# Sample attention values as 512-column products, and last expert products and final norm by thirds of tokens

## The reference, cut to what matters

```python
def mem_attend(q, mk, mv):
    s = jnp.einsum('bthd,bmhd->bhtm', q, mk.astype(q.dtype)).astype(jnp.float32) * (MEM_HEAD_DIM ** -0.5)
    p = jax.nn.softmax(s, axis=-1).astype(q.dtype)
    o = jnp.einsum('bhtm,bmhd->bthd', p, mv.astype(q.dtype))
    return o.reshape(q.shape[0], q.shape[1], MEM_Q)
```

```python
    x = x + peer(rmsnorm(x, norm_ffn_g), peer_w_q, peer_sub_keys, peer_u, peer_v)
...
def rmsnorm(x, g):
    xf = x.astype(jnp.float32)
    r = lax.rsqrt(jnp.mean(xf * xf, axis=-1, keepdims=True) + EPS)
    return (xf * r).astype(x.dtype) * g
```

## Time and profile before

| | us |
|---|---|
| median of three runs | 6134.89 |
| the profiled execution | 6135.75 |
| span of its records | 6134.0 |
| TensorE matmul busy | 5819.9 (95%) |
| VectorE busy | 3493.0 (57%) |
| ScalarE busy | 1329.1 (22%) |

### The profile page before, as it was taken

The page is one execution under the profiler, slowest core; times in us unless marked ns, Lnnn a source line. Parts: engine busy times, 40 slices in busy tenths (PEclk is TensorE's granted clock), DMA queues, the critical chain, the costliest instruction groups (busy, mean ns, idle before and its releaser), DMA issues. The chain is left out here.

```text
span 6134.0 us, 98920 instructions
## 1 busy us (share of the span) xinstructions
PE 5819.9 (95%) x37440; PEld 5687.3 (93%) x37440; DVE 3493.0 (57%) x8585; ACT 1329.1 (22%) x2383; POOL 875.0 (14%) x554
## 2 busy tenths in 40 slices
PE   8999999978887799899899999999999999999999
PEld 7999999878886599799899999999999999999998
DVE  3235300226664244599999998565565565565555
ACT  3113211213331013122233333121121121121121
POOL 0333223214332234133100000000000000000000
PEclk9999999979997799899999999999999999999999
DMA  4122222431110444211233333433333333333332
GB/s 153 59 73 94 97 90 94 145 111 35 35 35 14 144 148 125 75 59 48 80 149 146 142 141 139 136 87 101 83 87 100 83 90 98 83 92 96 83 92 69
DMA packets 706337, 584.63 MB, mean 95 GB/s; under 512 B 384664, under 2 KB 628376, under 8 KB 703189
## 3 DMA queue, kind: packets, MB, share of 16 engines
q1 hardware_dynamic: 663824, 425.64, 23.7%
q10 hardware_dynamic: 41184, 152.59, 7.0%
q0 software_dynamic: 1152, 4.19, 0.2%
HBM read 410.77 MB, written 171.59 MB: 95 GB/s over the span
## 5 line engine op out<-in xcount | busy, mean ns | idle before, releaser
L2959 DVE TENSOR_TENSOR yT<-yT,ex_y 128x352 f32<-128x352 f32 x1536 | 800.2, 521 | 918.6 <-PE ex_y L2851 918.6
L2213 PE MATMUL ea_banks<-h_high,ea_uT_high 128*128 128x352 f32 x3072 | 1013.8, 330 | 0.0
L2213 PE MATMUL ea_banks<-h_high,ea_uT_low 128*128 128x352 f32 x3072 | 991.8, 323 | 0.0
L2213 PE MATMUL ea_banks<-h_low,ea_uT_high 128*128 128x352 f32 x3072 | 991.6, 323 | 0.0
L2851 PE MATMUL ex_y<-ex_c_high,w_mb_high 128*128 128x352 f32 x3024 | 976.4, 323 | 3.7 <-DVE yT L2959 3.7
L2851 PE MATMUL ex_y<-ex_c_low,w_mb_high 128*128 128x352 f32 x3024 | 973.4, 322 | 0.0
L2851 PE MATMUL ex_y<-ex_c_high,w_mb_low 128*128 128x352 f32 x3024 | 972.2, 321 | 0.0
L120 PE MATMUL p_in<-h_high,w_in_high 128*128 128x352 f32 x2112 | 681.3, 323 | 0.0
L120 PE MATMUL p_in<-h_low,w_in_high 128*128 128x352 f32 x2112 | 676.9, 320 | 0.0
L120 PE MATMUL p_in<-h_high,w_in_low 128*128 128x352 f32 x2112 | 676.3, 320 | 0.0
L2213 PEld LDWEIGHTS ea_banks<-h_low,ea_uT_high 128*128 128x128 f32 x3072 | 584.4, 190 | 0.0
(11 more groups left out here) (470 smaller groups left out, 9851.5 us busy)
## 6 DMA issues: line engine op xcount, KB each, us to landing
ex_gate<-tmp_gates SPq DMA_DIRECT2D x128, 528.0 KB, 6.2
w_mb_raw<-in_peer_v SPq DMA_DIRECT2D x128, 512.0 KB, 5.6
ea_u_raw<-in_peer_u ACTq DMA_DIRECT2D x126, 512.0 KB, 3.3
w_in_raw<-in_w_in SPq DMA_DIRECT2D x88, 512.0 KB, 3.8
tmp_acts<-ea_coef ACTq DMA_DIRECT2D x64, 528.0 KB, 2.8
tmp_gates<-yT SPq DMA_DIRECT2D x11, 3072.0 KB, 9.0
tmp_gates<-sg_out SPq DMA_DIRECT2D x11, 3072.0 KB, 10.0
ex_kept<-tmp_acts SPq DMA_DIRECT2D x64, 528.0 KB, 6.9
```

Source lines behind the costliest of these rows:

```text
L2213: last = pe.matmul(acts.banks[:, n, 0:CH], a[:, c, :], b[:, c, chunk(n)], start=(c == 0 and a is acts.uT_high[s] and b is high), stop=(c = ...
L2959: dve.tensor_tensor(at, at, ps_y[:, n, 0:CH], ALU.add).then_inc(summed, 1)
```

## The change

In `attend`, the operands are exchanged. The cached values are the moving operand, 512 columns at a time, and the stationary operand is, for each sequence, a 128x128 block of probabilities that is zero outside that sequence's 16 rows (`s_pT` becomes [128, 8, 2, 128]; GpSimd zeroes it, VectorE copies the 16 columns of each sequence in). All 32 matmuls add into two banks of 128 rows by 1024 channels. The result then has rows of (sequence, head, token); it is copied to SBUF, transposed in 8 blocks, and 4 copies pick the 64 elements each that belong to a head.

In `experts`, the last pass takes its units chunk by chunk (all 8 channel blocks of 352 tokens, then the next chunk) and uses two banks in turn. The transposes of the final norm are put into it: a unit q of the first chunk is transposed in 3 pieces (128, 128 and 96 tokens) after unit q + 2, the second chunk's after units 15, 16 and 17, the third chunk's after unit 23. ScalarE squares each transposed tile with a running sum and takes its root, VectorE inverts and scales it between the sums of the next chunk, and SyncE stores it. `norm_rows_out` and its sums by matmul are gone, and with them a block.

```diff
-        s_pT = sb("s_pT", [P, MT, P])
+        s_pT = sb("s_pT", [P, NB, MT, P])
+        s_rows = sb("s_rows", [P, D])
...
-        s_values = banks[:, 6, 0:KT * NS].rearrange("p (c n) -> p c n", n=NS)
+        s_values = banks[:, 6:8, :]
+        s_columns = banks[:, 0:2, :].rearrange("p b (c n) -> p (b c) n", n=P)
...
+            pool.memset(s_pT[:, :, :, :], 0.0).then_inc(zeroed, 1)
             for t in range(tiles):
                 pool.wait_ge(out_kept, t + 1)
...
-                for c in range(KT):
-                    row = b * R + (c // 2) * TS
+                for half in range(2):
                     for m in range(MT):
-                        last = pe.matmul(s_values[:, c, b * TS:(b + 1) * TS], cache[:, b, m, c * P:(c + 1) * P],
-                                         s_pT[:, m, row:row + TS], start=(m == 0), stop=(m == MT - 1))
+                        last = pe.matmul(s_values[:, half, :], s_pT[:, b, m, :], cache[:, b, m, half * 512:(half + 1) * 512],
+                                         start=(b == 0 and m == 0), stop=(b == NB - 1 and m == MT - 1))
             last.then_inc(s_summed, 1)
+            pe.wait_ge(rows_kept, 2)
+            for c in range(KT):
+                last = pe.transpose(s_columns[:, c, :], s_rows[:, c * P:(c + 1) * P], k["ident"][:, :])
+            last.then_inc(rows_turned, 1)
...
-            dve.tensor_copy(s_pT[:, :, :], keys_bank(0)[:, 0:MT, :]).then_inc(soft, 1)
+            dve.wait_ge(zeroed, 2)
+            for b in range(NB):
+                last = dve.tensor_copy(s_pT[:, b, :, b * R:(b + 1) * R], keys_bank(0)[:, 0:MT, b * R:(b + 1) * R])
+            last.then_inc(soft, 1)
             dve.wait_ge(s_summed, 1)
-            dve.tensor_copy(s_o[:, :, :], s_values).then_inc(s_out_kept, 1)
+            dve.tensor_copy(s_rows[:, :], s_values.rearrange("p b n -> p (b n)")).then_inc(rows_kept, 2)
+            dve.wait_ge(rows_turned, 1)
+            for h in range(MH):
+                last = dve.tensor_copy(s_o[:, 2 * h:2 * h + 2, :].rearrange("p c (b t) -> p c b t", t=TS),
+                                       s_columns[:, 2 * h:2 * h + 2, :].rearrange("p c (b r) -> p c b r", r=R)[:, :, :, h * TS:(h + 1) * TS])
+            last.then_inc(s_out_kept, 1)
...
+        out_rows = [acts.u_raw[:, 0, :], acts.u_raw[:, 1, :], kept[:, 0:D]]
+        out_gain, out_squares = gate[:, 0, 0:D], acts.coef[:, 0, 0:D]
...
+        out_size = [P, P, CH - 2 * P]
+        LAST = 2 * pairs - 1
...
+        turned_after = {q + 2: (q,) for q in range(KT)}
+        turned_after.update({2 * KT - 1: range(KT, KT + 4), 2 * KT: (KT + 4, KT + 5), 2 * KT + 1: (KT + 6, KT + 7),
+                             3 * KT - 1: range(2 * KT, 3 * KT)})
+        def last_bank(q):
+            return (acts.banks[:, 2, 0:CH], ps_y[:, 0, 0:CH])[q % 2]
...
+            sp.wait_ge(coef_low, turn_of(LIVE, pairs - 1, 0) + 1)
+            sp.dma_start(out_gain, io["final_norm_g"].rearrange("o d -> (o d)").partition_broadcast(P)).then_inc(gain_in, 16)
+            for t in range(NT):
+                n, j = t // 3, t % 3
+                sp.wait_ge(out_scaled, t + 1)
...
+            def turn_out(q):
+                n, c = q // KT, q % KT
+                pe.wait_ge(summed, LAST * units + q + 1)
+                for j in range(3):
+                    if n and c == 0:
+                        pe.wait_ge(out_scaled, 3 * (n - 1) + j + 1)
+                    at = n * CH + j * P
+                    last = pe.transpose(out_banks[j][0:out_size[j], c, :], yT[:, c, at:at + out_size[j]], k["ident"][:, :])
+                    if c == KT - 1:
+                        last.then_inc(out_turned, 1)
+            def last_values():
...
+                for q in range(units):
+                    n, c = q // KT, q % KT
+                    pe.wait_ge(summed, LAST * units + q - 1)
...
+                    for earlier in turned_after.get(q, ()):
+                        turn_out(earlier)
...
+            for t in range(NT):
+                size = out_size[t % 3]
+                act.wait_ge(out_turned, t + 1)
+                act.activation(out_squares[0:size, :], out_banks[t % 3][0:size, :, :].rearrange("p c n -> p (c n)"), ACT.Square,
+                               accum_out=out_total[0:size, t:t + 1]).then_inc(out_squared, 1)
+                act.wait_ge(out_squared, t + 1)
+                act.activation(out_root[0:size, t:t + 1], out_total[0:size, t:t + 1], ACT.Sqrt, bias=k["eps"][0:size, 0:1],
+                               scale=1.0 / D).then_inc(out_rooted, 1)
...
+            def scale_out(t):
+                size = out_size[t % 3]
+                dve.wait_ge(out_rooted, t + 1)
+                dve.reciprocal(out_rinv[0:size, t:t + 1], out_root[0:size, t:t + 1]).then_inc(out_inverted, 1)
+                dve.wait_ge(out_inverted, t + 1)
+                if t == 0:
+                    dve.wait_ge(gain_in, 16)
+                if t >= 3:
+                    dve.wait_ge(out_stored[t % 3], 16 * (t // 3))
+                dve.scalar_tensor_tensor(out=out_rows[t % 3][0:size, :],
...
+            for n in range(NCH):
                 for c in range(KT):
...
+                    sum_last(n, c)
+                    if n and c in (3, 5, 6):
+                        scale_out(3 * (n - 1) + (c - 3) // 2 + (c == 6))
+            for t in range(NT - 3, NT):
+                scale_out(t)
...
-            norm_rows_out(nc, k, yT, io["final_norm_g"], io["out_y"])
```

More of the change, by code:

```diff
@@ L2839, in products, with values @@
                     act_chunk(pe, acts, high, low, e, s, n, first_chunk(g, s) + n)
-            def values(kind, m, coefs, first=False, v_high=wt.high, v_low=wt.low):
+            def values(kind, m, coefs, first=False):
                 pe.wait_ge(coef_low, coefs)
@@ L2849, in values @@
                     for s in range(2):
-                        for x, y in ((v_high[s], c_high[kind][s]), (v_high[s], c_low[kind][s]), (v_low[s], c_high[kind][s])):
+                        for x, y in ((wt.high[s], c_high[kind][s]), (wt.high[s], c_low[kind][s]), (wt.low[s], c_high[kind][s])):
                             last = pe.matmul(ps_y[:, n, 0:CH], x[:, c, :], y[:, chunk(n)],
-                                             start=(s == 0 and x is v_high[0] and y is c_high[kind][0]),
-                                             stop=(s == 1 and x is v_low[1]))
+                                             start=(s == 0 and x is wt.high[0] and y is c_high[kind][0]),
+                                             stop=(s == 1 and x is wt.low[1]))
@@ new lines, in last_values @@
+            def last_values():
+                pe.wait_ge(coef_low, 4 * pairs)
+                pe.wait_ge(v_low_made, 2 * LAST + 2)
+                pe.wait_ge(acts.chunk_kept, first_chunk(pairs - 1, 1) + NCH)
+                pe.wait_ge(acts.uT_low_made, 2 * STASHED)
+                for q in range(units):
+                    n, c = q // KT, q % KT
+                    pe.wait_ge(summed, LAST * units + q - 1)
+                    for s in range(2):
+                        for x, y in ((acts.uT_high[s], c_high[LIVE][s]), (acts.uT_high[s], c_low[LIVE][s]), (acts.uT_low[s], c_high[LIVE][s])):
+                            last = pe.matmul(last_bank(q), x[:, c, :], y[:, chunk(n)],
+                                             start=(s == 0 and x is acts.uT_high[0] and y is c_high[LIVE][0]),
+                                             stop=(s == 1 and x is acts.uT_low[1]))
+                    last.then_inc(multiplied, 1)
+                    for earlier in turned_after.get(q, ()):
+                        turn_out(earlier)
@@ L2874, in _ @@
             turn(pairs - 1, last=True)
-            values(LIVE, 2 * pairs - 1, 4 * pairs, v_high=acts.uT_high, v_low=acts.uT_low)
+            last_values()
         @block.scalar
@@ L3006, in _ @@
             sum_up(m, 20, units)
[L3007 to L3038, removed]
-                for c in range(KT):
[L3040 to L3080, removed]
-                dve.scalar_tensor_tensor(out=rows[0:size[t], t % SLOTS, :],
-                                         in0=ps[0:size[t], t % 2, :, :].rearrange("p b n -> p (b n)"),
-                                         scalar=rinv[0:size[t], t:t + 1], in1=gain[0:size[t], :],
-                                         op0=ALU.mult, op1=ALU.mult).then_inc(scaled, 1)
-        @block.sync
-        def _(sp):
-            sp.dma_start(gain[:, :], gain_dram.rearrange("o d -> (o d)").partition_broadcast(P)).then_inc(gain_in, 16)
-            for t in range(NT):
-                sp.wait_ge(scaled, t + 1)
-                sp.dma_start(dram[t * P:t * P + size[t], :], rows[0:size[t], t % SLOTS, :]).then_inc(stored[t % SLOTS], 16)
-            for s in range(SLOTS):
-                sp.wait_ge(stored[s], 16 * len(range(s, NT, SLOTS)))
@@ new lines, in sum_last @@
+            def sum_last(n, c):
+                q = n * KT + c
+                dve.wait_ge(multiplied, LAST * units + q + 1)
```

(7 more changed lines are left out.)

14 lines of the change are left out of this document (12 added, 2 removed).

## The result

The changed kernel takes 6087.92 us (median of four runs, 6084.72 to 6091.86), against 6134.85 before: a ratio of 0.9921 (0.9904 to 0.9938), 46.9 us less. I had forecast 6098.0 and a range of 6092 to 6107. The direction was right, 10 us of the gain were not in my sum, and the result lies 4 us outside the range.

The account below looks back on a forecast made before the run. TensorE's 54.78 us in the samples' attention and the final norm behind the experts' last sum were taken as on the path; gains of 22.1 and 14.8 us (36.9) from 6135.75, less 0.9 for the median, gave 6098.0, range 6092 to 6107.

Parts of the forecast that it names:

- my sum: Whole kernel: gains of 22.1 us in the samples' values and 14.8 in last pass and norm, 36.9 together.
- Samples' values, products 29.4 us: Samples' attention on TensorE: 64 records of 512 columns take 29.4 us (27.5 to 30.5), the clock returning after 3.8 us.
- Rival 1: Samples' values: the clock stays at half, products take 54.6 us, kernel 6123.4 us; chance 5%.
- The copies around them, 1.0 and 3.2 us: Samples' values: eight small copies before the products cost 1.0 us; copy, transposes and four copies after them 3.2.
- GpSimd's memset at nothing: Samples' attention: zeroing 2048 elements takes GpSimd 1.7 us but costs nothing, as it is idle there for 14.16 us.
- Last pass and norm, 14.8 us: Kernel's end: last store lands at 6118.8 instead of 6133.6, a gain of 14.8 us (ends 12 and 16).
- the stalls: Last expert pass: TensorE waits of 1.0, 1.8, 0.7 and 1.8 us behind VectorE's scalings and for the third piece's slot.
- Rivals 2: Final norm: ScalarE loads a table at each turn between square and root, 17.5 us more, kernel 6115.5; chance 3%.
- 3 (clock at 1.00): Samples' values and last pass: the full clock is lost in both, kernel slower at 6150.9 us; chance 2%.
- 4: Kernel's tail: only half hidden, VectorE blocks more or a table comes late, 6 us more, 6104; chance 8%.
- The blocks behind shift as they are: Blocks after the samples' attention: they only move earlier, with no change in their own times.

Follow-up runs that it names:

- values_128: Changed kernel with its products of the samples' values cut into 128 columns, 256 records instead of 64 of 512; one run, 6087.97 us.
- warm: Changed kernel with 16 and 8 identity transposes put into TensorE's idle gaps ahead of the products of the samples' values; 6086.02 us, ratio 0.9913.
- after_shift243: Changed kernel with 243 one-element memsets more in VectorE's list, in its wait for the samples' values; 6100.28 us, ratio 0.9939.
- before_shift16: Kernel before the change with 16 one-element memsets more in VectorE's list, in its wait for the samples' values; 6123.14 us, ratio 0.9976.
- tail_only: Changed kernel with the old `attend`, so only the last expert pass and final norm are changed; 6121.48 us, ratio 0.9976.
- samples_only: Kernel before the change with only the change's `attend`; 6100.68 us, ratio 0.9943.
- after_shift220: Changed kernel with 220 one-element memsets more in VectorE's list, in its wait for the samples' values; 6089.75 us, ratio 0.9925.
- after_shift242: Changed kernel with 242 one-element memsets more in VectorE's list, in its wait for the samples' values; 6101.77 us, ratio 0.9941.
- both: Changed kernel with identity transposes in the gaps ahead of the samples' products and an early root on ScalarE before the final norm; 6082.16 us, ratio 0.9913.

## Why the prediction was right or wrong

- *Samples' values, products 29.4 us:* 29.43, with the clock at half for 3.4 us. Right, and for the reason given: at half clock both forms cost the same (256 records at 0.21 us and 64 at 0.85), and `values_128` and `warm` show that the clock makes the gain. That it came out to 0.03 us is luck: other executions of the same products differ by up to 1.4. Rival 1 fell.
- *The copies around them, 1.0 and 3.2 us:* 0.9 and 3.1 (1305.73, the products' end, to the last copy's end at 1308.86). The stage gained 22.2 (22.1 forecast).
- *GpSimd's memset at nothing:* the products started 0.97 us behind the transposes, for VectorE's eight copies, and nothing waited for GpSimd. Right.
- *Last pass and norm, 14.8 us:* 15.1. Right to 0.3, in part by luck: the stalls were 3.7 us in all where the sum had 5.3, so the last store (issued at 6085.03, landing within 3.0) came 44.3 us behind the pass's first product where the sum had 45.7; but the span ended 1.8 us behind that landing, against 0.4 before by the earlier trace rows, and the sum had no term for this. Rivals 2 (one table load) and 3 (clock at 1.00) fell, and 4 as well.
- *"The blocks behind shift as they are":* **this is the step that failed.** `spread_gates` lost 18.3 us. I had read the gate stage's times nowhere, and took code that isn't edited for code that isn't changed. The runs showed in its place that the 13 instructions that the change adds to VectorE's list moved the loop behind them, so that its nine stops of 1.5 us ended. The 50 small fetches and the 13.5 us of "issue" in front of VectorE were in the trace of before, and I didn't look for them.

The check on the sum is `after_shift243`, in which the stall is kept: it gains 37.0 us against its own runs of before, where the sum said 36.9 (the interval of its ratio is 28 to 47 us, so that they agree to 0.1 is luck). The other way, 46.9 measured less 36.9 is 10.0, not 18.3. `before_shift16` gives 13.0 for the stall by itself, and `after_shift243` lies 12.4 above the changed kernel, so by the runs the stall is worth some 10 to 13 us of the kernel's time, while its stage shows 18. The intervals of the ratios are some 10 to 20 us wide, so each of these figures by itself is loose.

There is a pattern in them, though. For each kernel with more than one run I added up what its stages differ by from before, and compared that with the gain of its median. In `tail_only` and `after_shift243`, which keep the whole stall, the two agree to within 1 us. In the seven others (the changed kernel, `samples_only`, `before_shift16`, `after_shift220`, `after_shift242`, `warm` and `both`) the kernel gained 3 to 9 us less than its stages. So some of the stage's 18 us seems to be given back elsewhere. The traces show little of where: the stretch behind the stage is 0.8 us longer in the mean of the seven traces without the small fetches than in the five with them. The +4.3 and +6.3 us ahead of the stage vary from execution to execution by as much. Where the remainder goes stays open.

## What to carry to other kernels

A loop of a few hundred instructions on an engine can wait for its own code at each turn, and an edit far ahead of it can switch that on or off: it did here, on VectorE, with a loop of some 330 instructions. Before you credit or blame an edit, compare the stages that it doesn't touch, with their "issue" waits and the instruction queues; a handful of empty instructions in an idle stretch (16 here) can tell whether the place of the code is the cause. Price a change of a matmul's form in cycles at both clocks: here the form saved none, and the clock that came back with it saved 25 us (54.78 to 29.43).

## What I had not expected of the hardware

- VectorE's loop of some 330 instructions stopped for 1.4 to 1.5 us at a turn with its code in one place (before, `after_shift243`), 1.2 us with it one instruction earlier (`after_shift242`), and not at all 23 instructions earlier (`after_shift220`), where it fetched as often (51 packets).
- Each such stop of 1.5 us cost 2.0 us of the stage (18.3 in nine turns), since TensorE ran dry behind it and, at the turn shown, went to half clock for 6 us. With 242 memsets, nine stops of 1.2 us cost 1.5 each (13.7).
- A record of 4 moving columns took as long as one of 128 when both had a 128-column load and the clock was at half (0.21 us each).
- Matmuls of 4 columns and, with the operands exchanged, of 128, as many and with loads of the same size, differ in what the clock did: 54.8 us at 0.50 throughout, against 30.5 us with 0.50 in the first 3.5 only.
